# Decoder trunk on one core: the groups of a state-space core moved one projection tile earlier

## The reference

```
z, xBC, dt = split(h @ w_in)              # widths 2048, 3072 (x 2048, B 512, C 512), 32
xBC = silu(causal_conv4(xBC) + bias)      # depthwise, 4 taps
dt  = softplus(dt + dt_bias);  a = -exp(a_log)
# 4 groups of 8 heads of 64, state 128, two chunks of 128 tokens
y   = (C B^T * exp(segment sums of dt*a)) @ (x*dt) + C @ (state of chunk 0) * decay
y   = (y + d_skip * x) * silu(z)
y   = rms_norm(y in 4 groups of 512) * norm_w
x   = x + y @ w_out
```

## Time and profile before

| | |
|---|---|
| median of 3 runs | 1615.4 us (1615.35 to 1616.71) |
| the profiled execution's own time | 1616.62 us, granted clock 0.996 |
| its span, first to last instruction | 1614.6 us |
| TensorE busy | 1576.2 us, 98% of the span |
| VectorE, ScalarE, GpSimd busy | 1297.9, 1102.1, 92.5 us |
| mixer: first product of tile b to first product of out0 | 393.45 to 575.77 us |
| out0 to out3, then router to first expert product | 575.77 to 621.95, to 636.53 us |

### The profile page before, as it was taken

How to read it: one execution, slowest core, us unless ns; L and a number is a source line. 1 busy time by engine, 2 the same in 40 slices (tenths; PEclk the granted TensorE clock), 3 DMA queues, 4 the chain that set the end, 5 groups by cost and what they waited for, 6 DMA issues and landing times.

```text
span 1614.6 us, 24838 instructions
## 1 busy us (share of the span) xinstructions
PE 1576.2 (98%) x9155; PEld 1254.2 (78%) x9155; DVE 1297.9 (80%) x1568; ACT 1102.1 (68%) x1305; POOL 92.5 (6%) x69
## 2 busy tenths in 40 slices
PE   7999999999999999999999999999999999999997
PEld 7879999999998988676776776776776776776775
DVE  5676655556797765998999999999999998998996
ACT  5665544444754554778778778788778788788785
POOL 0001100100004200200000000000000000000000
PEclk9999999999999999999999999999999999999999
DMA  8325545455352258999999999999999999999980
GB/s 325 118 105 164 201 163 194 172 178 184 109 174 92 102 206 297 338 388 364 382 380 357 384 380 353 383 380 352 384 380 352 386 380 349 387 380 348 388 320 11
DMA packets 188258, 455.71 MB, mean 282 GB/s; under 512 B 4088, under 2 KB 4586, under 8 KB 188186
## 3 DMA queue, kind: packets, MB, share of 16 engines
q1 hardware_dynamic: 184938, 443.82, 75.2%
q0 software_dynamic: 2928, 10.17, 2.5%
q10 hardware_dynamic: 320, 0.73, 0.1%
HBM read 449.45 MB, written 5.26 MB: 282 GB/s over the span
## 4 chain that ended last, share of the span: by engine, by line
issue 56%; PE 35%; DVE 5%; POOL 2%; ACT 1%; DMA 0%; POOLq 0%; ACTq 0%; DVEq 0%
PE bank L696 34%; DVE split_mem L2080 1%; DVE split_mem L1595 1%; POOL out L662 1%; POOL mem L670 1%; DVE mem L1738 0%; POOL mem L634 0%; DMA rows<-norm_mix 0%; ACT split_mem L1178 0%; DVE mem L1772 0%; DVE mem L1622 0%; PE bank L721 0%; DVE mem L1784 0%; PE bank L995 0%; DVE mem L1749 0%
## 5 line engine op out<-in xcount | busy, mean ns | idle before, releaser
L696 PE MATMUL bank<-split_mem 128*128 128x256 f32 (+1 forms) x8064 | 1459.9, 341 | 14.8 <-DVE split_mem L1595 4.7
L696 PEld LDWEIGHTS bank<-split_mem 128*128 128x128 f32 (+1 forms) x8064 | 1140.4, 177 | 301.6 <-issue 9.9
L2080 DVE TENSOR_TENSOR split_mem<-mem,split_mem 128x1024 fp32r<-128x1024 f32 x668 | 811.6, 1229 | 80.2 <-ACT split_mem L1488 75.4
L1488 ACT CAST split_mem<-mem 128x1024 fp32r<-128x1024 f32 x672 | 705.7, 1052 | 203.7 <-PE bank L696 203.0
L1595 DVE TENSOR_TENSOR split_mem<-mem,split_mem 128x1024 fp32r<-128x1024 f32 x172 | 214.8, 1260 | 145.5 <-ACT split_mem L1178 145.4
L1178 ACT CAST split_mem<-mem 128x1024 fp32r<-128x1024 f32 x172 | 177.9, 1044 | 169.3 <-PE bank L696 165.9
L696 PE MATMUL bank<-mem 128*64 128x128 f32 (+7 forms) x376 | 40.3, 299 | 2.3 <-POOL mem L634 1.8
L662 POOL DMA_INDIRECT out<-mem,flag x8 | 11.6, 1452 | 533.5 <-ACT mem L1475 533.5
L1504 ACT ACTIVATE mem<-bank,small 96x512 f32<-96x512 f32 x56 | 38.3, 685 | 3.9 <-DVE small L2025 3.9
L2087 DVE TENSOR_TENSOR mem<-mem,bank 96x512 f32<-96x512 f32 x56 | 37.9, 676 | 0.0
L696 PEld LDWEIGHTS bank<-mem 128*64 128x64 f32 (+2 forms) x376 | 31.8, 163 | 7.5 <-issue 4.9
(11 more groups left out here) (195 smaller groups left out, 532.3 us busy)
## 6 DMA issues: line engine op xcount, KB each, us to landing
mem<-moe_w_gate SPq DMA_DIRECT2D x56, 2048.0 KB, 9.2
mem<-moe_w_up SPq DMA_DIRECT2D x56, 2048.0 KB, 9.2
mem<-moe_w_down SPq DMA_DIRECT2D x56, 2048.0 KB, 9.4
mem<-ssd_w_in SPq DMA_DIRECT2D x10, 2048.0 KB, 8.0
mem<-ffn_w_gate SPq DMA_DIRECT2D x7, 2048.0 KB, 8.4
mem<-ffn_w_up SPq DMA_DIRECT2D x7, 2048.0 KB, 7.9
mem<-ffn_w_down SPq DMA_DIRECT2D x7, 2048.0 KB, 7.8
mem<-attn_w_in SPq DMA_DIRECT2D x5, 2048.0 KB, 12.1
```

The source lines that it names most:

```text
L696: return nc.tensor.matmul(o, lhsT, rhs, start=start, stop=stop, skip_group_check=shared)
L1488: nc.scalar.copy(wsplit[:, EXPERT_BUFFER[n % SPLITS], 0, :].rearrange("p (k n) -> p k n", n=w.shape[2]), quarter(w, q)).then_inc(w_hi, 1)
L2080: tt_(lo, quarter(w, q), hi.bitcast(F32), ALU.subtract).then_inc(w_lo, 1)
```

## The change

The core of group g moves one tile earlier: into x3, z0, z1 and z2 (`CORE_AT`). For that, x3 is projected into banks 0 and 3 in place of 6 and 7, the group's inputs use banks 7, 6 and 4 (1 for the first group), and `xr` gets memory of its own inside the last group's z. The last two conv halves (10, 11) are finished in the rounds of z0 and z1. Tile z3 has no core beside it; the gates, squares, means and norms of groups 0 and 1 lie around it, and those of groups 2 and 3 inside out0 and out1. The `keep_busy` calls before the first y and before the last mean go. The dt chain is spread over the rounds of c and x0. The products of dt and of the router get 128 columns (the same values repeated) in place of 32 and 8. Three `keep_busy` products stand before the very first projection. ScalarE's table loads are written out (`preload_act_table`).

The diff, cut to its changed lines with a line of context:

```diff
-xr = dec[:, 0:2, :]
+xr = slot_mem(3)[:, 3072:4096].rearrange("p (b n) -> p b n", b=2)
...
 CONV_TILES = [("ssd_b", 0), ("ssd_c", 0)] + [("ssd_x", t) for t in range(4)]
+CORE_AT = {("ssd_x", 3): 0, ("ssd_z", 0): 1, ("ssd_z", 1): 2, ("ssd_z", 2): 3}
...
 B.plan(("ms", 2), 0), B.plan("dt", 1), B.plan("acs", 2)
-for i in range(12):
+for i in range(10):
...
 for g in range(GROUPS):
-    B.plan(("xn", g, 0), 1), B.plan(("cb", g), 0), B.plan(("xn", g, 1), 2)
-    B.plan(("z", g, 0), 0, ("ssd_z", g)), B.plan(("z", g, 1), 3, ("ssd_z", g))
+    B.plan(("xn", g, 0), 7), B.plan(("cb", g), 6), B.plan(("xn", g, 1), 4 if g else 1)
+    if g:
+        B.plan(("z", g - 1, 0), 0, ("ssd_z", g - 1)), B.plan(("z", g - 1, 1), 3, ("ssd_z", g - 1))
+    else:
+        B.plan(("conv", 10), 0, CONV_TILES[5]), B.plan(("conv", 11), 3, CONV_TILES[5])
...
         B.plan(("y", g, half), 1 + half)
+B.plan(("z", 3, 0), 0, ("ssd_z", 3)), B.plan(("z", 3, 1), 3, ("ssd_z", 3))
...
+        if g >= 2:
+            scale_z(g - 2)
...
                                 ALU.mult).then_inc(xw_ready, 1)
-        if g:
-            scale_z(g - 1)
...
                                     ALU.mult).then_inc(ce_ready, 1)
+    scale_z(GROUPS - 2)
...
-    def keep_busy(b, products, width=512):
+    def keep_busy(b, products, width=512, moving=cst):
...
         for _ in range(products):
-            mm(bank[b][:, 0:width], C("ident"), cst[:, 0:width], True, True)
+            mm(bank[b][:, 0:width], C("ident"), moving[:, 0:width], True, True)
...
             keep_busy(banks[0], 2)
+        if fresh == 0 and q == 0:
+            keep_busy(banks[0], 3, 512, xin[:, 0, :])
...
-    def down(acc, tile, first, last_tile):
+    def down(acc, tile, first, last_tile, between=None):
...
         for q in range(4):
+            if between:
+                between(q)
...
             for k in range(KD):
-                last = mm(bank[1][:, tt * SH:(tt + 1) * SH], xT[:, k, tt * P:(tt + 1) * P], wdt[:, k, :],
-                          k == 0, k == KD - 1)
+                last = mm(bank[1][:, tt * P:(tt + 1) * P], xT[:, k, tt * P:(tt + 1) * P],
+                          wdt[:, k, :].unsqueeze(1).broadcast_to([P, P // SH, SH]), k == 0, k == KD - 1)
...
             for b in range(4):
-                last = nc.tensor.transpose(bank[1 + c][:, b * P:(b + 1) * P],
+                last = nc.tensor.transpose(bank[B.at["xn", g, c][0]][:, b * P:(b + 1) * P],
...
                 for cc in range(TT):
-                    mm(bank[0][:, cc * P:(cc + 1) * P], BT[:, g, cc * P:(cc + 1) * P],
+                    mm(bank[6][:, cc * P:(cc + 1) * P], BT[:, g, cc * P:(cc + 1) * P],
...
                        CT[:, g, cc * P:(cc + 1) * P], True, True)
-                B.finish(nc.tensor.transpose(bank[0][:, T:T + P], BT[:, g, 0:P], C("ident")), ("cb", g))
-    for t, tile in enumerate(CONV_TILES):
-        if tile == CONV_TILES[-1]:
-            group_inputs(0)
+                B.finish(nc.tensor.transpose(bank[6][:, T:T + P], BT[:, g, 0:P], C("ident")), ("cb", g))
+    for t, tile in enumerate(CONV_TILES[:-1]):
...
                 step_products()
-            if t == 2 and q == 3:
+            if t == 2 and q == 0:
...
-    for g in range(GROUPS):
-        if g:
-            group_inputs(g)
+    for tile, g in CORE_AT.items():
+        group_inputs(g)
...
         for hf in range(2):
-            B.claim(pe, ("z", g, hf))
+            B.claim(pe, ("z", g - 1, hf) if g else ("conv", 10 + hf))
...
         for q in range(2):
-            project(("ssd_z", g), (0, 3), q)
+            project(tile, (0, 3), q)
...
         B.claim(pe, ("state", g))
+        B.released(pe, ("cb", g))
...
         for q in range(2, 4):
-            project(("ssd_z", g), (0, 3), q)
+            project(tile, (0, 3), q)
...
             B.claim(pe, ("y", g, half))
-            if g == 0 and half == 0:
-                keep_busy(1, 3)
...
             B.finish(last, ("y", g, half))
-    for g in range(GROUPS):
+    def mean_of_group(g):
...
         B.claim(pe, ("y_ms", g))
-        if g == 3:
-            keep_busy(7, 5)
+    for hf in range(2):
+        B.claim(pe, ("z", 3, hf))
+    for q in range(4):
+        if q == 0:
+            mean_of_group(0)
+        if q == 3:
+            mean_of_group(1)
+        project(("ssd_z", 3), (0, 3), q)
+    def later_means(q):
+        if q == 1:
+            mean_of_group(2)
+        if q == 2:
+            mean_of_group(3)
...
     for g in range(GROUPS):
-        down("ssd_acc", ("ssd_out", g), g == 0, g == 3)
+        down("ssd_acc", ("ssd_out", g), g == 0, g == 3, later_means if g == 1 else None)
...
             for tt in range(TT):
-                last = mm(bank[4][:, tt * E:(tt + 1) * E], xT[:, k, tt * P:(tt + 1) * P], router[:, k, :],
+                last = mm(bank[4][:, tt * P:(tt + 1) * P], xT[:, k, tt * P:(tt + 1) * P],
+                          router[:, k, :].unsqueeze(1).broadcast_to([P, P // E, E]),
...
         act.wait_ge(y_ready, g + 1)
+        if g in (1, 2):
+            dense_tile_end(act, ("ssd_z", 3))
...
         if before == ("ssd_c", 0):
-            ssd_decays()
+            act.wait_ge(w0_arg, 1)
+            fn(w0, w0, ACT.Exp).then_inc(w0_ready, 1)
+            conv_silu(0)
...
             i = CONV_TILES.index(before)
-            if i == 2:
-                act.wait_ge(w0_arg, 1)
-                fn(w0, w0, ACT.Exp).then_inc(w0_ready, 1)
...
             if i:
+                if i == 5:
+                    nc.scalar.preload_act_table(ACT.Silu)
...
                 conv_first_tap(i, (2 * i, 2 * i + 1))
+                if i == 5:
+                    logs_and_exps()
...
             copy_z(before[1])
-        if before == ("ssd_z", GROUPS - 1):
-            gate_silu([GROUPS - 1])
-            logs_and_exps()
+        if before == ("ssd_z", 0):
+            nc.scalar.preload_act_table(ACT.Silu)
+            conv_silu(10)
+        if before == ("ssd_z", 2):
...
             y_rms(0)
-            gated_squares([GROUPS - 1])
-            for g in range(1, GROUPS):
-                y_rms(g)
-                y_hi(g - 1)
-        if before == ("ssd_out", 0):
-            y_hi(GROUPS - 1)
+        if before == ("ssd_z", 3):
+            y_hi(1)
...
             squares(2)
+        if before == ("ssd_z", 2):
+            gated_squares([1])
+        if before == ("ssd_z", 3):
+            nc.scalar.preload_act_table(ACT.Silu)
+            gate_silu([2, 3])
+        if before == ("ssd_out", 0):
+            y_rms(2)
...
         split(n + 1, 0)
+        if before == ("ssd_z", 0):
+            conv_silu(11)
+            logs_and_exps()
+        if before == ("ssd_z", 1):
+            nc.scalar.preload_act_table(ACT.Silu)
+            gate_silu([0, 1])
+            logs_and_exps()
+        if before == ("ssd_z", 2):
+            y_hi(0)
+        if before == ("ssd_out", 0):
+            y_hi(2)
+            y_rms(3)
...
         if (kind, t) == ("ssd_c", 0):
-            conv_silu(0)
-        if before in CONV_TILES and before != ("ssd_b", 0):
+            ssd_decays()
+        if before in CONV_TILES[1:-1]:
...
             conv_silu(2 * CONV_TILES.index(before))
-        if (kind, t) == ("ssd_z", 0):
-            conv_silu(11)
-        if kind == "ssd_z":
-            core(t)
-            if t == GROUPS - 1:
-                gate_silu(range(t))
-                gated_squares(range(t))
+        if (kind, t) == ("ssd_x", 3):
+            logs_and_exps()
+        if (kind, t) in CORE_AT:
+            core(CORE_AT[kind, t])
+        if before == ("ssd_z", 1):
+            gated_squares([0])
+        if before == ("ssd_z", 2):
+            y_rms(1)
+        if before == ("ssd_z", 3):
+            gated_squares([2, 3])
+            logs_and_exps()
+        if before == ("ssd_out", 0):
+            y_hi(3)
...
         for c in range(TT):
-            last = stt(out=dtv[:, c, :], in0=bank[1][:, c * SH:(c + 1) * SH], scalar=rstd[:, T + c:T + c + 1],
+            last = stt(out=dtv[:, c, :], in0=bank[1][:, c * P:c * P + SH], scalar=rstd[:, T + c:T + c + 1],
+    def decays():
...
             dve.wait_ge(taps_done, i - 1)
-        B.release(per_token(two(xr[:, i % 2, :]), two(bank[4 + i % 4][:, :])), ("conv", i))
+        B.release(per_token(two(xr[:, i % 2, :]), two(bank[B.at["conv", i][0]][:, :])), ("conv", i))
...
             B.release(tt_(xd[:, g % 2, c * 512:(c + 1) * 512].rearrange("p (h d) -> p h d", d=HD),
-                          bank[1 + c][:, :].rearrange("p (h d) -> p h d", d=HD),
+                          bank[B.at["xn", g, c][0]][:, :].rearrange("p (h d) -> p h d", d=HD),
...
                 tt_(cbm[:, g % 2, :].rearrange("p (c l) -> p c l", l=P),
-                    bank[0][:, 0:T].rearrange("p (c l) -> p c l", l=P),
+                    bank[6][:, 0:T].rearrange("p (c l) -> p c l", l=P),
...
                     C("upto").unsqueeze(1).broadcast_to([P, TT, P]), ALU.mult).then_inc(cbm_ready, 1)
```

(95 more changed lines are left out.)

## The result

The changed kernel takes 1606.26 us (median of 4 runs, 1605.16 to 1607.12), the kernel before beside it 1616.06 (4 runs, 1615.35 to 1617.70). The ratio is 0.9937, with an interval from 0.9924 to 0.9950: faster by 0.63%, three times the 0.2% within which the prediction calls a difference no change. The forecast was 1602.0 within 1596.5 to 1608.5. The median lies in that range, 4.3 us above the forecast and 0.8 us above the likeliest case's own bounds (1598 to 1605.5). The gain is 9.8 us by the medians, and 11.0 by the two traces (spans of 1614.6 and 1603.6), against 13.3 forecast.

What follows compares the result with a forecast made beforehand. TensorE bounds the experts, so time saved ahead arrives undiminished; mixer gaps, unread products and half clock are the stock. Mixer 16.8 - 6.7 = 10.1, router 1.4, start 1.8: 13.3 off 1615.4 gives 1602, range 1596.5 to 1608.5.

Steps and rivals of the forecast that it cites:

- x1: Mixer tile x1: reordering the dt chain removes a 1.92 us gap and the half-clock stretch behind it, winning 3.5 us.
- The other terms of the 16.8: Mixer waits and unread products removed: 1.8 us before z1, z2 and z3, 4.5 at the first y, 7.0 at the means.
- x3: Mixer tile x3, now beside core 0: VectorE becomes the limit there and holds TensorE back 1.2 us (0.4 to 2.0).
- z1: Mixer tile z1: core(2) starts late through VectorE and ScalarE order, costing 0.9 us; one instruction blocked beside GpSimd, 1.3 more.
- z2: Mixer tile z2: core(3) starts 4.1 us late, costing TensorE 1.4 us; one instruction blocked beside GpSimd, 1.3 more.
- Table loads: ScalarE's loads priced at the trace's 1.28 us; the skill page's extra 1.38 each would add 4.1 for three, giving 1606.2.
- Router: Wider router products keep the clock up, so the 16 transposes behind them take half; 1.4 us won.
- Start: First projection quarter: three added 512-column products fill the gap before it, bringing full clock earlier; 1.8 us won.
- rival 2: Mixer core tiles run later than laid out or the clock falls there: 6 us more lost, 1608; chance 17%.
- 1: Expert part: weight loads set the pace, so only 2.3 us would be won, 1613; chance 6%.
- 3: Mixer core tiles: GpSimd stops VectorE throughout, making the kernel slower, 1631; chance 6%.
- 4: Mixer: expected stalls in x3, z1 and z2 don't come and the clock holds, 20 us won, 1595.4; chance 12%.

## Why the prediction was right, and where it was off

**The frame** was right. The experts pass on what is saved ahead of them (0.41 us of difference), and the stock was gaps, half clock and waits in the mixer. The kernel before without its dummy products showed that these lay in waits.

**x1** was sized at 3.5 and gave 3.65 (x3's group inputs start at 456.19 against 460.00, less the 0.16 of before tile b). Undoing the order shows that 1.9 of it is the wait. The other 1.6 is the clock's fall, and the same wait without a fall shows that it doesn't come each time.

**The other terms of the 16.8**: the waits ahead of the first y and the last mean are confirmed by the kernel without its dummy products, and the 0.47 us before z1 and z2 are gone in the trace. No experiment takes the gaps of x3 and out0 apart.

**x3** 1.2 forecast, 0.41 + 0.35 + 0.68 = 1.44 measured; **z0** nothing, as forecast; **out0** 0.6 and 0.77; no wait at the means, as forecast.

**z1 is the term that was mis-sized**: 0.9 for the order plus one blocked instruction of 1.3, 2.2 us in all, against 4.07. The order was about right: with z scaling cut down 1.12 stay, 0.74 of it before the first y. The blocking was not one instruction but three: two of taps 10 (1.92 us) and one of the core's products (1.07), 2.95 in all by the trace without them. The two causes share one slack, so the share of each depends on which is taken out first: the order alone taken out gives 2.0. **z2** was wrong the other way: 1.4 + 1.3 forecast, 1.38 measured, and none of it from the z scaling. So "2.6 for blocking" came out near (2.95) in total by luck and wrong in each place. The Trainium skill ("GPSIMD Engine Reference", the table of specifications) says that the two engines contend where VectorE has two SBUF inputs; the taps, which read two, fit it, and so do the subtractions, which read PSUM and stay at 4.22 us for 16 beside GpSimd. It is the runs that show the size: a tap ends only when GpSimd's product has ended.

**Mixer**: held back 1.44 + 4.07 + 1.38 + 0.77 = 7.66 against 6.7 forecast. 16.8 - 7.66 = 9.1, and the trace has 9.29 to the router (10.1 forecast).

**Table loads**: the next instruction starts 0.01 us behind the 1.28 of the load (510.05, 511.34). The further drain of 1.38 us of the Trainium skill ("ScalarE: Activation LUTs", What ACT_TABLE_LOAD costs) doesn't appear on ScalarE, and the order in z1 held 1.12 us in all, as the trace's price gave. The price by the trace was the right one. By the page the total would have been 1606.2, and 1606.26 was measured; that is a coincidence, since the drain that the page adds isn't there.

**Router**: 1.4 forecast, 1.14 measured, transposes under 2 us as said. But I took the half clock behind the narrow products as given, from one trace. Without any change there it was absent in the kernel before without its dummy products (13.34 us from router to experts), and in the changed kernel the narrow form cost 2.8 us and 1.5 more behind dt. What the wide form is worth is thus between nothing and 4.3 us, by the execution that it is compared with. dt I had put at a cost of 0.1 and no gain.

**Start**: 1.8 forecast, 1.33 measured at 18.26, of which the added products give 0.7. Then it was lost: it was still there at 111.68 (113.00 before), and the clock's fall behind the wait that follows took it. In the two traces of the same code in which the clock holds there it arrives: tile b begins at 391.13 and 391.34, 2.1 to 2.3 us ahead of before. I priced falls as a rival (2) and not as something that an earlier start can run into. This and z1 make up the miss: 1.6 at the start, 0.8 in the mixer, 0.3 at the router, less 0.4 in the experts, 2.3 us of the span (13.3 against 11.0); by the medians the gain is 1.2 less again (9.8).

**Rivals**: 1 fell (later loads, same time). 3 fell (z's scaling costs 2.95 us in all). 4 didn't come. 2 came in part: one stall grew by 1.9, and the clock fell once, at 112 us and not in the core tiles. The forecast of 1602 was 4.3 us too low, and it is the range, made wide enough for most of rival 2, that holds the result.

## What to carry to other kernels

Where work of GpSimd comes to lie beside VectorE's products from SBUF, count each instruction that overlaps as stopped, and look where it lands, not how much there is: three of them cost 2.95 us in z1, and two in z2 (a gate product of 2.29 us in place of 1.23, a split of 2.28 in place of 1.24) cost nothing, for the core was done. When delays stand in a row on the way to one wait, take the slack off their sum once; each repair is then worth its full size until the slack is reached. A gain ahead of a wait of 1.6 us may be lost to the clock behind it; a few products in the wait keep it.
